# A modulation computed in four single-tile steps, with TensorE started on zeros and the products of a tile split by operand

## The reference

```python
mx = [m[:, None, :] for m in jnp.split(jax.nn.silu(c) @ w_mod[l] + b_mod[l], 6, axis=-1)]
mc = jnp.split(jax.nn.silu(c_ctx) @ w_mod[l] + b_mod[l], 6, axis=-1)
hx = modulate(rmsnorm(x, g_norm1[l]), mx[0], mx[1])     # h * (1 + scale) + shift
hc = modulate(rmsnorm(ctx, g_norm1[l]), mc[0], mc[1])
px = jnp.split(hx @ w_in[l], IN_SPLIT_IDX, axis=-1)
pc = jnp.split(hc @ w_in[l], IN_SPLIT_IDX, axis=-1)
```

## Time and profile before

| | |
|---|---|
| median of three runs | 823.16 us (822.74 to 824.34) |
| span of the profiled execution | 821.9 us |
| around the span, against the median | 1.3 us |
| TensorE busy | 797.3 us, 97% of the span |
| VectorE, ScalarE, GpSimd busy | 428.3, 418.8, 376.9 us |
| bytes moved, mean rate | 146.61 MB, 178 GB/s |

### The profile page before, as it was taken

How to read it: one execution, slowest core, us unless ns; L and a number is a source line. 1 busy time by engine, 2 the same in 40 slices (tenths; PEclk the granted TensorE clock), 3 DMA queues, 4 the chain that set the end, 5 groups by cost and what they waited for, 6 DMA issues and landing times.

```text
span 821.9 us, 14292 instructions
## 1 busy us (share of the span) xinstructions
PE 797.3 (97%) x5493; PEld 695.4 (85%) x5493; DVE 428.3 (52%) x684; ACT 418.8 (51%) x641; POOL 376.9 (46%) x181
## 2 busy tenths in 40 slices
PE   6999999999899999999999999999999999999996
PEld 4778877887778999999998889999887988899985
DVE  4675568984667533422336747645455333423435
ACT  5335426455846444444444955654756544444443
POOL 3126000000164654666545986565464554666452
PEclk9999999999999999999999999999999999999999
DMA  9984577134953666555654796434455556566551
GB/s 320 302 285 133 161 235 253 54 102 103 345 168 116 198 193 190 175 179 185 192 166 132 227 205 186 130 105 132 150 167 167 157 182 197 180 190 191 184 149 51
DMA packets 94397, 146.61 MB, mean 178 GB/s; under 512 B 15742, under 2 KB 64111, under 8 KB 94353
## 3 DMA queue, kind: packets, MB, share of 16 engines
q1 hardware_dynamic: 92896, 143.23, 55.9%
q0 software_dynamic: 1424, 2.77, 1.3%
q10 hardware_dynamic: 32, 0.01, 0.0%
HBM read 144.93 MB, written 1.06 MB: 178 GB/s over the span
## 4 chain that ended last, share of the span: by engine, by line
PE 85%; DVE 6%; issue 3%; POOL 2%; ACT 2%; DMA 2%; DVEq 0%; SPq 0%; ACTq 0%; POOLq 0%
PE bank L1877 82%; POOL w_lo L628 2%; ACT w_hi L693 1%; PE bank L2147 1%; PE bank L1968 1%; DMA raw<-in_w_mod 1%; DMA x<-in_x 1%; DMA gate_mlp_b<-gate_rows 1%; DVE x L1829 1%; PE bank L2455 1%; DVE w_lo L1196 1%; DVE stat L1513 1%; DVE x L1642 0%; DVE o_lo L1734 0%; DVE bank L1641 0%
## 5 line engine op out<-in xcount | busy, mean ns | idle before, releaser
L628 POOL TENSOR_TENSOR w_lo<-raw,w_hi 128x1024 fp32r<-128x1024 f32 (+2 forms) x150 | 361.8, 2428 | 318.7 <-ACT w_hi L693 318.5
L693 ACT ACTIVATE w_hi<-raw 128x1024 fp32r<-128x1024 f32 (+1 forms) x218 | 226.1, 1045 | 217.3 <-PE bank L1877 192.5
L1196 DVE TENSOR_TENSOR w_lo<-raw,w_hi 128x1024 fp32r<-128x1024 f32 x71 | 87.0, 1236 | 141.3 <-ACT w_hi L693 141.2
L1877 PE MATMUL bank<-z_hi,w_hi 128*128 128x256 f32 x384 | 109.0, 284 | 0.2
L1877 PE MATMUL bank<-z_hi,w_lo 128*128 128x256 f32 x384 | 107.2, 279 | 0.0
L1877 PE MATMUL bank<-z_lo,w_hi 128*128 128x256 f32 x384 | 107.1, 279 | 0.0
L1877 PE MATMUL bank<-n_hi,w_hi 128*128 128x256 f32 x352 | 100.4, 285 | 1.0 <-POOL w_lo L628 1.0
L1877 PE MATMUL bank<-n_hi,w_lo 128*128 128x256 f32 x352 | 99.8, 284 | 0.0
L1877 PE MATMUL bank<-n_lo,w_hi 128*128 128x256 f32 x352 | 99.0, 281 | 0.0
L1877 PE MATMUL bank<-w_hi,mlp_h_hi 128*128 128x512 f32 x216 | 85.3, 395 | 0.0
L1877 PE MATMUL bank<-w_hi,mlp_h_lo 128*128 128x512 f32 x216 | 85.2, 395 | 0.0
(11 more groups left out here) (419 smaller groups left out, 1553.0 us busy)
## 6 DMA issues: line engine op xcount, KB each, us to landing
raw<-in_w_in SPq DMA_DIRECT2D x54, 512.0 KB, 4.5
raw<-in_w_down SPq DMA_DIRECT2D x54, 512.0 KB, 3.7
raw<-in_w_gu SPq DMA_DIRECT2D x44, 512.0 KB, 3.5
raw<-in_w_up SPq DMA_DIRECT2D x32, 512.0 KB, 3.7
raw<-in_w_mod SPq DMA_DIRECT2D x24, 512.0 KB, 4.1
raw<-in_w_mod SPq DMA_DIRECT2D x32, 256.0 KB, 6.1
raw<-in_w_out SPq DMA_DIRECT2D x12, 512.0 KB, 4.0
raw<-in_w_in SPq DMA_DIRECT2D x8, 336.0 KB, 3.0
```

The costliest lines, as they stand in the source:

```text
L628: nc.gpsimd.tensor_tensor(wl[:, w % SPL, 0:size], raw[:, slot_raw, 0:size], wh[:, w % SPL, 0:size].bitcast(F32), ALU.subtract).then_inc(s_ ...
L693: nc.scalar.activation(wh[:, w % SPL, 0:size], raw[:, slot_raw, 0:size], ACT.Copy).then_inc(s_hi, 1)
L1196: V.tensor_tensor(wl[:, w % SPL, :], raw[:, slot_raw, :], wh[:, w % SPL, :].bitcast(F32), ALU.subtract).then_inc(s_lod, 1)
L1877: return nc.tensor.matmul(out_, l, r_, start=start, stop=stop, skip_group_check=True)
```

## The change

The first four channel tiles get their shift and scale one tile at a time. Their parts of `w_mod` (1 MB for each tile, as eight transfers of 128 KB with runs of 128 numbers) no longer go through the ring but into tiles that are not in use yet (`mod_early`). The remaining four stay two groups of two tiles, in the ring. `MODS` lists six steps: first tile, number of tiles, first chunk.

TensorE begins with four products of zeros. The 1/rms of the 256 tokens and of the 256 context tokens are made apart. The table of ScalarE is one that holds both Ln and Exp. For tiles 0 to 3 the products go by operand (`forget(k, product)` and `query(k, product)`): first high by high, then what needs `wl`, then what needs `hl`, with the modulation of the next tile between. Rows of a single tile are copied by ScalarE (`row_copy`), those of a group by VectorE as before. The scale is made from PSUM with a prepared bias, `h` is given on for the two halves of the tokens apart.

```diff
         FF_AT, HQ_AT, FB_AT = 1792, 768, 2304
-        add_mod(0)
         for j in range(4):
             add_in(2 * j, 2, FF_AT, 512)
-            if j < 3:
+            add_in(2 * j, 2, HQ_AT, 512)
+            if j in (1, 2):
                 add_mod(j + 1)
-            add_in(2 * j, 2, HQ_AT, 512)
...
+        MODS = ((0, 1, 0), (1, 1, 2), (2, 1, 4), (3, 1, 6), (4, 2, 8), (6, 2, 12))
+        EARLY = 8
...
+            def mod_tile(k):
+
+                for half in range(2):
+                    dst = mod_early(2 * k + half).rearrange("p (k s n) -> p k s n", k=4, s=2)
+                    for j in range(4):
+                        sp.dma_start(dst[:, j], mod_pairs[:, 4 * half + j, :, P * k:P * k + P]).then_inc(s_early[2 * k + half], 16)
+
+            mod_tile(0)
             for n, (kind, parts) in enumerate(chunks):
+                if n == 2:
+                    mod_tile(1)
+                    mod_tile(2)
+                elif n == 4:
+                    mod_tile(3)
...
-            load_functions(LN)
+            load_functions(LN_EXP)
+
+            def row_copy(m):
+
+                act.wait_ge(s_mod, MODS[m + 1][2])
+                nc.scalar.activation(modrow[:, m % 2, 0:T], ps[6][:, 0:T], ACT.Copy).then_inc(AC.sem, AC.tick(f"row {m}"))
...
+                if t % 2:
+                    if t == 3:
+                        row_copy(0)
+                    act.wait_ge(AC.sem, AC[f"sq {t}"])
+                    ln_exp(act, 67 + t, 63 + t, 2, D, f"1 {t // 2}")
 
             for k in range(KT):
                 if k == 0:
                     hi(1)
+                elif k == 1:
+                    for v in (1, 0):
+                        act.wait_ge(PE.sem, PE[f"x rstd {v}"])
+                        nc.scalar.activation(rowb[:, T * v:T * v + T], ps[FACTORS[v]][:, 0:T], ACT.Copy).then_inc(AC.sem, AC.tick(f"x rstd {v}"))
+                    hi(2)
+                    row_copy(1)
+                elif k == 3:
+                    row_copy(3)
+                    hi(4)
                 elif k == 2:
+                    row_copy(2)
+                    hi(3)
+                elif k == 4:
                     act.wait_ge(DV.sem, DV["lb max"])
...
-                act.wait_ge(DV.sem, DV[f"h {k}"])
                 for v in range(2):
...
+                    act.wait_ge(DV.sem, DV[f"h {k} {v}"])
...
+            def modulation(m, lows=()):
+
+                k0, n, _ = MODS[m]
+                if n == 2:
+                    dve.wait_ge(s_mod, MODS[m][2] + 4)
+                    tick(V.tensor_copy(modrow[:, m % 2, :], ps[6][:]), f"row {m}")
                 for w in lows:
                     chunk_lo(w, number["w"][w] % RAW)
...
+                dve.wait_ge(PE.sem, PE[f"mod t {m}"])
...
+            for k in (2, 3):
+                modulation(k, (2,) if k == 2 else ())
+                h_product(k, k)
+                h_low(k)
...
+            pe.wait_ge(DV.sem, DV["csil 0"])
+            for _ in range(4):
+                mm(ps[0][:, 0:T], csil[:, 0:4, :].rearrange("p k n -> p (k n)"), csil[:].rearrange("p k n -> p (k n)"), True)
...
+            keep_clock(1, 2)
             pe.wait_ge(s_x, 16)
...
+            x_factors(0)
             pe.wait_ge(DV.sem, DV["csil"])
-            mod_rows(0, (0,))
+            mod_rows(0)
             pe.wait_ge(s_in, 11 * 16)
...
             pe.wait_ge(DV.sem, DV["cols"])
             mod_cols(0)
+            x_factors(1)
             pe.wait_ge(DV.sem, DV["xT 1 3"])
-            keep_clock(0, 2)
-            mod_rows(1, (0,))
+            keep_clock(0, 1)
...
+            for k in range(4):
+                if k % 2 == 0:
+                    pe.wait_ge(s_hi, k + 1)
+                pe.wait_ge(AC.sem, AC[f"hh {k} 1"])
...
+                    forget(k, 0)
+                if k < 3:
+                    mod_rows(k + 1, (0,))
+                split(k // 2 * 2)
+                forget(k, 1)
+                pe.wait_ge(DV.sem, DV[f"hl {k}"])
+                ins = forget(k, 2, (0, 1))
+                if k < 3:
+                    mod_rows(k + 1, (1,))
+                ins = forget(k, 2, (2, 3))
...
+                if k % 2 == 0:
+                    pe.wait_ge(s_hi, k + 2)
+                query(k, 0)
+                query(k, 1, (0, 1))
+                if k < 3:
+                    mod_cols(k + 1)
+                query(k, 1, (2, 3))
+                split(k // 2 * 2 + 1)
+                ins = query(k, 2)
...
+                if k == 3:
+                    mod_rows(4)
+            w_at[0] = 4
+            mod_cols(4)
+            for j in range(2, 4):
```

More of the change, by code:

```diff
@@ L375, in program @@
         s_mod = sem("mod_used")
+        s_early = [sem(f"mod_early_in{c}") for c in range(EARLY)]
         s_acc = sem("acc_used")
@@ L1215, in x_from_psum @@
                                    ps[XT_BANKS[v][pair]][:].rearrange("p (k t) -> p k t", k=2)), f"xT {v} {pair}")
[L1217 to L1224, removed]
-                    ins = V.tensor_scalar(dg4[:, t, :], ident, stat[:, 68 + t:69 + t], None, ALU.mult)
[L1226 to L1231, removed]
+            for pair in range(4):
+                x_from_psum(0, pair)
@@ L1239, in modulation @@
[L1239 to L1243, removed]
+                dve.wait_ge(PE.sem, PE[f"mod t {m}"])
+                at_ = 160 + 4 * k0
+                for k in range(k0, k0 + n):
+                    c = at_ + 2 * (n + k - k0)
+                    ins = V.tensor_scalar(modc[:, 8 + k, :], ps[7][:, c:c + 2], stat[:, 240 + k:241 + k], cols[:, R_G1 + k:R_G1 + k + 1],
+                                          ALU.add, ALU.mult)
@@ L1245, in h_product @@
+                tick(ins, f"modc scale {m}")
+                for k in range(k0, k0 + n):
+                    c = at_ + 2 * (k - k0)
+                    ins = V.tensor_scalar(modc[:, k, :], ps[7][:, c:c + 2], cols[:, R_BMOD + k:R_BMOD + k + 1], None, ALU.add)
+                tick(ins, f"modc {m}")
+            def h_product(k, m):
                 if k >= 4:
                     own(f"hl {k - 4}")
+                own(f"modc scale {m}")
                 for v in range(2):
                     c = slice(T * v, T * v + T)
-                    ins = V.scalar_tensor_tensor(out=hf[:, k % 4, c], in0=xT(k)[:, c], scalar=modc[:, 8 + k, v:v + 1],
-                                                 in1=rowb[:, c], op0=ALU.mult, op1=ALU.mult)
@@ L1924, in _, with row_made @@
             nc.tensor.transpose(ps[7][:, 0:16], rowsc[0:16, :], ident[0:16, 0:16]).then_inc(PE.sem, PE.tick("c rows"))
[L1926 to L1936, removed]
-                for half in halves:
-                    for j in range(2):
-                        arrived(pe, number["mod"][4 * g + 2 * half + j])
+            def row_made(m):
+                if MODS[m][1] == 1:
+                    pe.wait_ge(AC.sem, AC[f"row {m}"])
+                else:
+                    pe.wait_ge(DV.sem, DV[f"row {m}"])
@@ new lines, in mod_cols, with mod_rows @@
+            def mod_cols(m):
+                k0, n, _ = MODS[m]
+                row_made(m)
+                for q in range(2 * n):
+                    at_ = 160 + 4 * k0 + 2 * q
+                    ins = mm(ps[7][:, at_:at_ + 2], modrow[:, m % 2, P * q:P * q + P], cst[:, C_SEL:C_SEL + 2], True)
+                ins.then_inc(PE.sem, PE.tick(f"mod t {m}"))
+            def mod_rows(m, halves=(0, 1)):
+                k0, n, c0 = MODS[m]
+                if m:
+                    row_made(m - 1)
+                for half in halves:
+                    if n == 1:
+                        pe.wait_ge(s_early[c0 + half], 4 * 16)
+                    else:
+                        for j in range(n):
+                            arrived(pe, number["mod"][c0 - EARLY + n * half + j])
@@ L1946, in mod_rows @@
+                        ins = mm(ps[6][32 * strip:32 * strip + 32, 0:T * n], csil[:, k, :], w, half == 0, half == 1)
+                        if strip == 3 or (n == 2 and strip == 1):
                             ins.then_inc(s_mod, 1)
@@ L2019, in _, with forget @@
             to_hq = [(ps[4 + j // 2][:, T * (j % 2):T * (j % 2) + T], j % 2 == 0) for j in range(4)]
-            keep_clock(0, 2)
-            for j in range(4):
+            def forget(k, product, tiles=range(HG)):
+                s = (2 * (k // 2)) % SPL
+                l, r_ = ((wh, hh), (wl, hh), (wh, hl))[product]
+                for h in tiles:
+                    c = 512 * (k % 2) + P * h
+                    ins = mm(ps[h][:], l[:, s, c:c + P], r_[:, k, :], k == 0 and product == 0, False)
+                return ins
```

114 lines of the change are left out of this document (72 added, 42 removed).

## The result

The changed kernel takes 836.64 us (834.57 to 838.14, 4 runs) against 822.95 us for the kernel before on the same chip: slower by 13.7 us by the medians. The ratio over all runs is 1.0156, with a 95% interval of 1.0138 to 1.0175. The forecast was 829.9 with a range up to 835.0: the direction was right, the size was half of what came, and the time lies outside the range. The profiled execution took 836.07 us with a span of 834.3.

The account below looks back on a forecast made before the run. TensorE was taken to bound the kernel: start -5.2, moved work +2.4, holes +10.6, old waits -1.1 give +6.7, so 823.2 became 829.9 us. The range was 826 to 835.

Parts of the forecast that it names:

- The bound: TensorE, busy 97% of the span, sets the time; a shift of k = 4 from 44.80 us is passed on.
- The start: First product of the forget gate at 16.8 us instead of 22.04, a gain of 5.2 us.
- the lower of the two bounds: Arrival of tile 0's weights at the rate of 1 KB runs: 12.3 us, against 12.8 forecast and 15.3 upper.
- The rival of the late tile: Short runs cost as much as long ones, tile 0 in at 15.3: 834.2 us, chance 0.10.
- The zeros: Zero products at the beginning raise TensorE's clock; without that effect the start is 0.5 us later.
- The holes: Seven TensorE waits from k = 1 up to k = 4, together 10.6 us against 1.1 before.
- The operand chain is hidden: Rival: the chain from columns to operand lies under products, four holes go: 822.5 us, chance 0.12.
- The work moved behind the start: Rows, columns and tiles between first product and k = 4 take 24.1 us, 2.4 more than before.
- about 1.1 of waits: TensorE waits of the kernel before between 22.04 and 44.80 us, subtracted from the new holes.
- The clock falls in the last hole: Rival: after the 3.2 us wait before k = 4 products run at half speed, costing 2.6: 832.5 us, chance 0.10.
- as they are needed: The last group's weights, fetched from near 45 us, come by about 55 us, with no wait.
- around the span: The 1.3 us by which the runs' median exceeds the profiled span, added to reach 829.9 us.

Follow-up runs that it names:

- e6: Changed kernel, same operations reordered: whole next rows behind the first operand, next columns behind the second, ScalarE's high parts before row copies; 824.50 us.
- e10: e6 with the 704 KB of constants put behind the weights of step 5; 822.27 us, ratio to the kernel before 0.9989.
- e4: Changed kernel without the four products of zeros and the two products before the tokens; 836.56 us.
- e8: Kernel before, with only the four products of zeros and the two products before the tokens added; 823.23 us.
- e2: Changed kernel with useless products filling TensorE's holes before k = 1 to 4; 832.83 us.
- e1: Changed kernel with seven useless products between the columns of step 4 and the first product of k = 4; 834.87 us.
- e3: Changed kernel with the rows and columns of step 4 moved among the products of k = 3; 832.46 us.
- e7: Changed kernel with only the TensorE order of e6, ScalarE left as in the changed kernel; 826.97 us.
- e9: e2 with the 704 KB of constants put behind the weights of step 5; 831.61 us.
- e5: Changed kernel with ScalarE making the high parts of chunks 2 and 3 before the row copies instead of behind; 831.18 us.
- e11: e10 with six useless products in the remaining waits up to k = 4; 821.81 us, ratio to the kernel before 0.9982.

## Why the prediction was wrong

**The step that failed.** In the sum of the prediction the granted clock stood at nothing: every product was priced at the higher level, and a fall was only a rival (0.10, in the last hole, 2.6 us). It fell twice and cost 1.5 + 2.4 = 3.9 us. A second term was too small: the work put between the products, by 1.8 us. The other terms held to 0.4 us.

**The bound: right for a delay.** A later TensorE before `k = 4` was passed on in full: 44.80 to 55.11 is 10.3 us, the slow clock behind 55.11 adds 2.4, and the profiled spans differ by 12.4. Downstream work took up no more than 0.3. For an earlier TensorE the bound does not hold: in e6 and e10 `k = 4` is 2.7 and 2.6 us before, and the weights of step 5 and of chunk 6 take part of it.

**The start: right in number, by another path.** 17.21 for 16.8, a gain of 4.8. The last transfer of tile 0 landed at 13.1 (forecast 12.8), 2.9 us behind the context tokens, about what 1 MB takes at the rate of 1 KB runs (3.0), the lower of the two bounds; between 10 and 20 us 5589 packets of 617 bytes in the mean moved at 345 GB/s. The rival of the late tile (15.3) is refuted. But the chain of the changed kernel does not go through tile 0:

```profile
1.68 8.52 DMA ctx_rows<-in_ctx
...
10.24 1.97 PE bank L2044 x16
```

The context tokens, put at 9.3, landed at 10.2 in this execution, and TensorE came to the rows of tile 0 at 12.6, only shortly before its last transfer was in. Eight profiles with this start have the first product 6.9 to 7.2 us behind the landing of the context tokens, at 16.2 to 17.2. So the number was met with some luck: one arrival came 0.9 late, and it was the one that counted.

The zeros were given 0.5 us. The times show nothing of it (e4, e8); the start in e4's profile hints at 0.7.

**The holes: right in place and size.** Forecast 1.2, 2.1, 1.2, 1.0, 0.9, 1.0, 3.2; idle time of TensorE in the profile 1.1, 1.9, 0.8, 0.8, 0.5, 0.8, 3.3, 9.2 for 10.6 (the forecast counts from the moment when the next product could start, the profile from the end of the last one, 0.17 later each; counted alike it is 10.3 for 10.6). That VectorE waits for GpSimd showed again: the two halves of `h 3` took 1.38 with the `w_lo` beside them, 0.88 otherwise, and ScalarE took up the first half at 42.66, 0.3 behind GpSimd's end at 42.35.

```profile
40.00 2.35 POOL L650 TENSOR_TENSOR w_lo<-raw,w_hi 128x1024 fp32r<-128x1024 f32 x1 [32.30 <-ACT w_hi L715]
...
41.65 1.38 DVE L1296 SCALAR_TENSOR_TENSOR h_f<-x_T_a,mod_cols,mod_rows_b 128x256 f32<-128x256 f32 x2
```

That the order is the cause of the loss is shown by e6: same operations, 12.1 us less. "The operand chain is hidden" was refuted by the waits themselves.

**The work moved behind the start: the term was too small.** I priced a half of a tile's rows at 0.5 and nothing for going from products to rows and back. The timeline of the changed kernel:

```profile
18.88 1.20 PE L1935 MATMUL bank<-h_hi,w_lo 128*128 128x512 f32 x4
...
19.91 0.63 PE L1935 MATMUL bank<-h_lo,w_hi 128*128 128x512 f32 x2
...
20.47 0.64 PE L1935 MATMUL bank<-hg_level_keys,c_silu 128*32 128x256 f32 x8
...
21.04 0.74 PE L1935 MATMUL bank<-h_lo,w_hi 128*128 128x512 f32 x2
```

Four products take 1.03 (0.93 priced), two take 0.56 (0.47), the rows 0.57 (0.5). Each insertion of rows is dearer by some 0.27, with six of them 1.6 us. By tiles it is 1.8: from the first product of `k = 1` to that of `k = 2` are 8.39 us, less the wait of 1.91 and the way of 0.17 this is 6.3, for 5.7 priced, and three tiles have it. e2, with no slow stretch, has 36.4 us from its first product (16.36) to `k = 4` (52.80), for 34.7 forecast: 1.7. Splitting the rows of a tile into halves and putting them into the middle of the products was a cost by itself. The kernel before shows the price too:

```profile
24.68 0.40 PE L1877 MATMUL bank<-h_hi,w_lo 128*128 128x512 f32 x1
25.01 1.07 PE L1877 MATMUL bank<-raw,c_silu 128*32 128x512 f32 x8
26.01 0.50 PE L1877 MATMUL bank<-h_hi,w_hi 128*128 128x512 f32 x1
26.34 0.39 PE L1877 MATMUL bank<-h_lo,w_hi 128*128 128x512 f32 x1
```

The products before and behind the rows take 0.33 from start to start instead of 0.233. In the prediction this lay hidden in the "about 1.1 of waits" before `k = 4`: the profile has one wait of 0.57 there.

**The clock.** "The clock falls in the last hole" had a chance of 0.10, because waits of 1.6 us did not show it before. It fell twice, and first already behind the wait of 1.9 that ends at 33.1. That fall lasts from 33.3 to 36.7 and costs 1.5: the same instructions take 5.33 us behind 33.12 (to 38.45) and 3.87 behind 24.73 (to 28.60). From 55.11 to 60.5 TensorE takes 5.4 for what took 2.95 before (44.80 to 47.75, first product to first rows of step 5), 2.4 more; the rival had 2.6. The Trainium skill (TensorE: Matmul & The Clock Gate, "HAM oscillation — how this bites in real kernels") says that waits between bursts of products bring the clock down, with waits of about 3 to 5 us in its example. The trace agrees for the second fall, behind 3.27 us; the first came behind 1.91, which that example does not cover. I gave the order of the changed kernel, with a wait of 3.2 in its own forecast, too small a chance for it. e1 and e2 show the cost: filling the waits with useless products gives back 1.8 and 3.8 us.

**The weights of step 5: a bound I put as "as they are needed".** They were two microseconds late. In the changed kernel the slow clock covered that; with most repairs it came up as a wait of 1.5 to 2.3 (e1, e2, e3, e6, e7). The constants in the middle of them are the cause of that wait: put behind, it is gone in both profiles (e9, e10), and the next chunks are late by 0.3 instead.

**The account.** Forecast +6.7; start +0.4; holes -0.3; insertions +1.8; first fall +1.5; second fall +2.4: +12.5, and the profiled executions differ by 12.4 in span. The medians differ by 13.7, 1.3 more. Of this 0.6 is the changed kernel's profiled execution, which lies below its median (836.07 for 836.64). The other 0.7 is an estimate for the kernel before: in the runs that have both numbers the time is about 1.8 us above the span, so its span of 821.9 belongs to a time near 823.7, above the median 822.95. The 1.3 "around the span" of the prediction was therefore no property of the kernel, but that does not touch the forecast of +6.7.

## What to carry to other kernels

An earlier start is worth nothing if the order behind it has no work to lay over the next operand: before interleaving finer, write down for each chain (rows, copy, columns, scale, operand) its length and the products behind its last step in TensorE's own order. A wait of about 2 us on TensorE can cost more than its length, since the work behind it can run at half speed: of the ten waits of 1.9 us and more between 17 and 62 us in these profiles, nine had a fall of the clock in them or just behind. Fill them with work, or if there is none with products of no use. Changing between kinds of products in the middle of a stream has a price at each change, so insert in few large pieces. A late transfer can stay hidden behind a slower stage, so after each repair read the waits again before judging the next.

## What the runs showed of the hardware that was not expected

- The clock fell behind a wait of 1.91 us in four profiles (the changed kernel, e1, e3, e4) and not behind one of 1.96 in e2, where the waits before the tiles were filled, nor behind one of 1.10 in the place of the 1.91 (e5), nor in the kernel before behind one of 1.6. So the wait alone does not decide; what TensorE did around it, or chance, has a part.
- A fall near 16 us, during the first products, is there in the profiles of e3, e4, e7 and e9 and not in those of the changed kernel, e1, e2, e5, e6 and e10, with the same wait of 0.8 before the first product in all ten. It costs about 1.5 us (tile 0 takes 8.96 in e3 and 7.52 in the changed kernel). That it is what makes executions of one kernel differ by 2 to 4 us (e3: 830.26 to 834.05, the slowest being the profiled one) is likely and not shown.
- Products of zeros raise the clock like any other. The eight records of zeros take 3.78 us in e10, and the four of the same shape with constants right behind them 1.13. Without both (e4) the first tokens' transposes take 421 ns each, with them 16 transposes took 1.97 us, 0.12 each:

```profile
7.49 1.97 PE L2044 MATMUL bank<-cst,x 128*128 128x128 f32 x16 [0.81 <-DMA x<-in_x]
```

- The column of the granted clock reads 1.00 during the slow transposes of the kernel before and of e4 too: at the very start it doesn't show the level, and the durations have to tell. e11 has both: at a granted clock of 0.50 the same transposes take 421 ns.
